# The down product of the ConvFFN as seven block products over pairs of token tiles, with the weight rows in three groups

## The reference

```
def conv_ffn(h, conv_state, w_up, w_conv, b_conv, w_down):
    u = h @ w_up                                   # (T, 1024) @ (1024, 5632)
    ...                                            # causal depthwise convolution of width 3 over tokens
    a, g = jnp.split(uc, 2, axis=-1)
    out = (jax.nn.silu(a) * g) @ w_down            # (T, 2816) @ (2816, 1024)
    return out, padded[:, -(CONV_W - 1):]
...
    x = x + g2 * f_out
```

## Time and profile before

| what | value |
|---|---|
| median of three runs | 3029.07 us |
| the profiled execution's own time, as the page gives it: its span | 3031.5 us |
| TensorE busy | 2948.6 us, 97% |
| VectorE busy | 1759.8 us, 58% |
| ScalarE, GpSimd busy | 1207.0 and 586.9 us |
| matmuls of the down product on TensorE | the first starts at 2504.5, the last at 3020.1 us |

### The profile page before, as it was taken

One profiled execution on the slowest core, in us unless ns is written; L12 is line 12 of the kernel. 1 busy time (PEld: TensorE's weight loads), 2 busy tenths in 40 slices (PEclk: granted clock), 3 DMA queues, 4 the chain that ended last, 5 costly groups with the idle time before them and its releaser, 6 DMA issues.

```text
span 3031.5 us, 48232 instructions
## 1 busy us (share of the span) xinstructions
PE 2948.6 (97%) x17353; PEld 2562.3 (85%) x17353; DVE 1759.8 (58%) x2649; ACT 1207.0 (40%) x2325; POOL 586.9 (19%) x609
## 2 busy tenths in 40 slices
PE   7999999999999999899998999999999999999998
PEld 5878888887777888888888999999999998887886
DVE  2300016733998999795667777777877775234222
ACT  4611112223776888454554333333423233113110
POOL 3310003312666777220110000000000000002000
PEclk8999999999999999999999999999999999999999
DMA  6322224544522251796654444444666676335331
GB/s 217 112 79 73 72 70 157 159 133 112 132 58 58 59 103 36 233 322 204 197 181 171 154 152 153 153 150 157 189 208 217 207 235 233 130 116 186 130 127 55
DMA packets 321026, 446.38 MB, mean 147 GB/s; under 512 B 68994, under 2 KB 220360, under 8 KB 314086
## 3 DMA queue, kind: packets, MB, share of 16 engines
q1 hardware_dynamic: 304616, 394.94, 41.1%
q0 software_dynamic: 14928, 49.38, 4.8%
q10 hardware_dynamic: 1332, 0.06, 0.0%
HBM read 289.20 MB, written 155.10 MB: 147 GB/s over the span
## 4 chain that ended last, share of the span: by engine, by line
PE 51%; DVE 4%; DMA 2%; issue 1%; ACT 1%; SPq 0%; DVEq 0%; ACTq 0%; POOL 0%
PE facc L2600 26%; PE dacc L2709 15%; PE eacc L2579 6%; DMA w_out_plain<-w_out 1%; PE mpT L2726 1%; PE mpm L2735 1%; PE eyT L2562 0%; PE mpS L2745 0%; PE exT L2592 0%; DVE drows L2306 0%; PE mpT L2776 0%; DVE fV L2238 0%; DMA fraw<-w_up 0%; DMA dring<-w_down 0%; PE mpN L2761 0%
## 5 line engine op out<-in xcount | busy, mean ns | idle before, releaser
L2709 PE MATMUL dacc<-drows,dact 128*128 128x512 f32 (+1 forms) x2200 | 511.1, 394 | 4.7 <-DVE dact L2312 1.2
L2709 PEld LDWEIGHTS dacc<-drows,dact 128*128 128x128 f32 (+1 forms) x2200 | 407.8, 186 | 107.6 <-POOL drows L1783 3.2
L767 PE MATMUL pacc<-pring,h1H 128*128 128x512 f32 x1360 | 431.9, 394 | 3.4 <-ACT h1H L326 3.4
L2600 PE MATMUL facc<-fright,fsums 128*128 128x416 f32 x2112 | 417.8, 353 | 9.6 <-ACT facc L1846 6.6
L2600 PEld LDWEIGHTS facc<-fright,fsums 128*128 128x128 f32 x2112 | 398.0, 189 | 15.4 <-issue 7.3
L1123 DVE TENSOR_TENSOR_SCAN aC<-aB,aC,a 128x512 f32<-128x512 f32 (+3 forms) x326 | 362.8, 1113 | 12.1 <-ACT aB L1079 1.1
L1183 POOL TENSOR_TENSOR aS<-aS,aC 128x512 f32<-128x512 f32 (+3 forms) x326 | 335.1, 1036 | 151.9 <-DVE aC L1123 145.5
L767 PEld LDWEIGHTS pacc<-pring,h1H 128*128 128x128 f32 x1360 | 256.8, 189 | 56.2 <-ACT h1H L326 3.5
L2600 PE MATMUL facc<-fright,fwH 128*128 128x416 f32 x1056 | 290.2, 356 | 8.8 <-DVE fU L2222 6.9
L1750 POOL DMA_DIRECT2D y_out<-dy x34 | 18.5, 543 | 1383.3 <-DVE dy L2329 1383.3
L767 PE MATMUL pacc<-pring,h1L 128*128 128x512 f32 x640 | 248.0, 389 | 0.0
(11 more groups left out here) (329 smaller groups left out, 4976.7 us busy)
## 6 DMA issues: line engine op xcount, KB each, us to landing
sums_d<-fsums SPq DMA_DIRECT2D x88, 512.0 KB, 2.9
fsums<-sums_d SPq DMA_DIRECT2D x88, 512.0 KB, 4.7
dact_plain<-act_d SPq DMA_DIRECT2D x32, 1408.0 KB, 6.4
fraw<-w_up SPq DMA_DIRECT2D x66, 512.0 KB, 4.1
proj_out<-pstage SPq DMA_DIRECT2D x119, 256.0 KB, 2.0
qk_T<-pturn POOLq DMA_DIRECT2D x68, 256.0 KB, 3.1
mwa<-w_ada SPq DMA_DIRECT2D x16, 1024.0 KB, 6.8
aq<-qk_T SPq DMA_DIRECT2D x28, 512.0 KB, 11.9
```

The lines of the kernel that those rows point to most:

```text
L767: op = mm_(acc[:, n % NB], h[:, kk, tok(t)], weight(q, w), start=(j == 0), stop=(j == len(order) - 1))
L2600: mm = nc.tensor.matmul(bank, a[:, kk], b[:, kk], start=(begins and kk == 0 and m == 0), stop=(kk == count - 1 and m == 2), skip_group_che ...
L2709: mm = nc.tensor.matmul(down_acc[0:rows, n % 2], at[:, l, kk, 0:rows], r, start=(kk == 0 and m == 0), stop=(kk == NF - 1 and m == len(pass ...
```

## The change

The sixteen prompt tiles are taken in pairs (p, p + 8), the output columns in halves, and the weight rows in three groups of 6, 8 and 8 blocks (GROUPS; half of a group is s = 3, 4, 4 blocks). For one group and one pair the product is a 2 by 2 block product, which Strassen's scheme does in seven products instead of eight. That is a "unit"; there are 3 x 8 = 24 (UNITS), group by group. A product of a unit has 3s matmuls of 128x512, all into one PSUM bank.

Left operands of a unit are A11, A12, A22 and four sums S1 to S4 of activation blocks, each 128 x (128s): VectorE makes the sums (left_sum_of), ScalarE the high and VectorE the low halves, a unit ahead. Right operands ("cells") of a group are B11, B21, B22 and T1 to T4, four sums of weight blocks, each 128 x (512s). GpSimd makes T1 to T4 (first_sums for group 0, next_sum for the others), ScalarE the high halves, VectorE the low halves (for group 0, GpSimd those of T3 and B22, cell_rest). The cells of the next group are made in the last unit of a group (change) and in the first of the next (changed).

ScalarE copies pass the banks on (down_seed_b, down_seed_c, take_five). finish_out gates a result out of PSUM; a partial result is added by GpSimd (add_residual) onto the residual, which is loaded from x1_d and stored there again for each of the three groups, the last time to y_out. SyncE issues all of them. The activations of unit w + 2 are loaded when all low halves of unit w + 1 are made, since all units but unit 1 use one buffer (part). VectorE's convolution and product of the last up tile move into unit 0. The sample is multiplied in plain fp32: 88 matmuls (sample_down, after units 4, 6 and 13), 32 rows each, four of them side by side in the columns of the array with 256 output columns each.

```diff
@@ shapes, orders and places @@
-    NR = 6
-    ND = 2 * NT
-    SWITCH = NT
+    GROUPS = ((0, 3), (6, 4), (14, 4))
+    HALF = NPT // 2
+    UNITS = len(GROUPS) * HALF
+    UP = 2 * NF
+    PRODUCTS = ("P1", "P5", "P6", "P2", "P7", "P3", "P4")
...
@@ SyncE: a unit's loads and stores @@
+            def load_act(w):
+                g, p, k0, s = unit(w)
+                if w == 2:
+                    sp.wait_ge(left_low, 7)
+                elif w > 2:
+                    sp.wait_ge(left_low, 7 * w)
+                to = part_first if w == 1 else part
+                for e in range(2):
+                    sp.dma_start(to[:, e, 0:2 * s], d["act_d"][p + HALF * e, :, k0:k0 + 2 * s, :]).then_inc(part_in, 16)
+            def load_res(w, j):
+                at_least(sp, res_stored[j], 16 * w)
+                rows_, cols_ = out_place(w, j)
+                sp.dma_start(res_of(w, j), d["x1_d"][rows_, cols_]).then_inc(res_in[j], 16)
+            def store_out(w, j):
+                if w == UNITS - 1 and j > 1:
+                    sp.wait_ge(last_out, j - 1)
+                else:
+                    sp.wait_ge(out_ready, 4 * w + j + 1)
+                rows_, cols_ = out_place(w, j)
+                sp.dma_start(d["y_out" if unit(w)[0] == 2 else "x1_d"][rows_, cols_], res_of(w, j)).then_inc(res_stored[j], 16)
...
+                store_out(w, 0)
+                store_out(w, 1)
+                if w + 1 < UNITS:
+                    load_res(w + 1, 0)
+                store_out(w, 2)
+                if w + 1 < UNITS:
+                    load_res(w + 1, 1)
+                if w + 2 < UNITS:
+                    load_act(w + 2)
+                store_out(w, 3)
+                if w + 1 < UNITS:
+                    load_res(w + 1, 2)
+                    load_res(w + 1, 3)
@@ GpSimd @@
+            def add_residual(w, j):
+                if w == UNITS - 1 and j > 1:
+                    return
+                pool.wait_ge(down_gated, 4 * w + j + 1)
+                pool.wait_ge(res_in[j], 16 * w + 16)
+                nc.gpsimd.tensor_tensor(res_of(w, j), res_of(w, j), y2_of(w, j), ALU.add).then_inc(out_ready, 1)
+            def first_sums():
+                sub = lambda to, x, y: nc.gpsimd.tensor_tensor(to, x, y, ALU.subtract)
+                t1, t2, t3, t4 = (cells_plain[f"T{n}"][:, :, 1] for n in range(1, 5))
+                pool.wait_ge(first_blocks_in, 144)
+                for n in range(3):
+                    op = sub(t1[:, n], b12_rows[n], cells_plain["B11"][:, n, 1])
+                op.then_inc(cell_sum, 1)
+                pool.wait_ge(b22_in, 48)
+                pool.wait_ge(cell_sum, 1)
+                pool.wait_ge(done["P6"], UP)
+                sub(cell("T2", 0)[2], cell("B22", 0)[2], cell("T1", 0)[2]).then_inc(cell_sum, 1)
...
+            def cell_rest(name, g):
+                pool.wait_ge(cell_high, 7 * g + HIGHS[g].index(name) + 1)
+                pool.wait_ge(cell_sum, 4 * g + 4)
+                top, low, _ = cell(name, g)
+                nc.gpsimd.tensor_tensor(low, cell_source(name, g), top.bitcast(F32), ALU.subtract).then_inc(cell_low_pool, 1)
+            def next_sum(n, g):
+                sub = lambda to, x, y: nc.gpsimd.tensor_tensor(to, x, y, ALU.subtract).then_inc(cell_sum, 1)
+                if n == 0:
+                    pool.wait_ge(sample_done, g + 1)
+                    pool.wait_ge(done["P5"], UP + HALF * g)
+                    sub(cell("T1", g)[2], raw_block("B12", g), raw_block("B11", g))
+                elif n == 1:
+                    pool.wait_ge(cell_sum, 4 * g + 1)
+                    pool.wait_ge(done["P6"], UP + HALF * g)
+                    sub(cell("T2", g)[2], raw_block("B22", g), cell("T1", g)[2])
+                elif n == 2:
+                    pool.wait_ge(cell_sum, 4 * g + 2)
+                    pool.wait_ge(*low_of("B11", g))
+                    sub(raw_block("B11", g), raw_block("B21", g), cell("T2", g)[2])
+                else:
+                    sub(raw_block("B12", g), raw_block("B22", g), raw_block("B12", g))
+            def down_slot(w):
+                g, p = unit(w)[0:2]
+                change = p == HALF - 1 and g + 1 < len(GROUPS)
+                if change:
+                    next_sum(0, g + 1)
+                    next_sum(1, g + 1)
+                add_residual(w, 0)
+                if change:
+                    next_sum(2, g + 1)
+                add_residual(w, 1)
+                add_residual(w, 2)
+                if change:
+                    next_sum(3, g + 1)
+                add_residual(w, 3)
...
+            first_sums()
+            cell_rest("T3", 0)
+            cell_rest("B22", 0)
+            for w in range(UNITS):
+                down_slot(w)
@@ ScalarE @@
+            def down_seed_b(w):
+                act.wait_ge(done["P1"], UP + w + 1)
+                at_least(act, down_gated, 4 * w)
+                copy(down_b, down_a).then_inc(seeded_b, 1)
+            def take_five(w):
+                act.wait_ge(done["P5"], UP + w + 1)
+                act.wait_ge(c12_taken, UP + w)
+                act.wait_ge(c22_taken, UP + w)
+                copy(five(w), down_e).then_inc(e_taken, 1)
+            def down_seed_c(w):
+                act.wait_ge(done["P6"], UP + w + 1)
+                act.wait_ge(c12_taken, UP + w)
+                copy(down_c, down_b).then_inc(seeded_c, 1)
+            def down_slot(w):
+                g, p = unit(w)[0:2]
+                change = p == HALF - 1 and g + 1 < len(GROUPS)
+                changed = p == 0 and g > 0
+                down_seed_b(w)
+                if changed:
+                    cell_high_of("T3", g)
+                take_five(w)
+                if change:
+                    cell_high_of("B11", g + 1)
+                down_seed_c(w)
+                if changed:
+                    cell_high_of("B22", g)
+                if w + 1 == UNITS:
+                    return
+                for name in LEFTS:
+                    if name == "S3":
+                        if w == 0:
+                            silu(UP - 1, NARROW)
+                        if change:
+                            cell_high_of("T1", g + 1)
+                    elif name == "S4" and change:
+                        cell_high_of("B21", g + 1)
+                    elif name == "A22" and change:
+                        cell_high_of("T2", g + 1)
+                    elif name == "A12" and changed:
+                        cell_high_of("T4", g)
+                    left_high_of(name, w + 1)
@@ VectorE @@
...
+            def left_sum_of(n, w):
+                at = act_blocks(w)
+                s1, s2, s3, s4 = (left(f"S{m}", w)[2] for m in range(1, 5))
+                if n == 1:
+                    dve.wait_ge(part_in, 32 * w + 32)
+                    dve.wait_ge(done["P5"], UP + w)
+                    op = v.tensor_tensor(s1, at["A21"], at["A22"], ALU.add)
+                elif n == 2:
+                    dve.wait_ge(done["P2" if w == 0 else "P6"], UP + w)
+                    dve.wait_ge(left_sum, 4 * w + 1)
+                    op = v.tensor_tensor(s2, s1, at["A11"], ALU.subtract)
...
+                op.then_inc(left_sum, 1)
+            def left_low_of(name, w):
+                dve.wait_ge(left_high, 7 * w + LEFTS.index(name) + 1)
+                if name in ("S1", "S2"):
+                    dve.wait_ge(left_sum, 4 * w + (2 if name == "S1" else 4))
+                top, low, own = left(name, w)
+                v.tensor_tensor(low, own if name[0] == "S" else act_blocks(w)[name], top.bitcast(F32), ALU.subtract).then_inc(left_low, 1)
...
+            def finish_out(w, j):
+                y_ = y2_of(w, j)
+                gate_ = down_gate[:, out_place(w, j)[1]]
+                dve.wait_ge(done[("P2", "P7", "P3", "P4")[j]], UP + w + 1)
+                at_least(dve, out_ready, 4 * w + j - 1)
+                if j in (0, 3):
+                    v.tensor_tensor(y_, down_a if j == 0 else down_b, gate_, ALU.mult).then_inc(down_gated, 1)
+                else:
+                    sem = c22_taken if j == 1 else c12_taken
+                    dve.wait_ge(e_taken, UP + w + 1)
+                    v.tensor_tensor(y_, down_b if j == 1 else down_c, five(w), ALU.add).then_inc(sem, 1)
+                    dve.wait_ge(sem, UP + w + 1)
+                    v.tensor_tensor(y_, y_, gate_, ALU.mult).then_inc(down_gated, 1)
...
+            def down_slot(w):
+                g, p = unit(w)[0:2]
+                n = w + 1
+                more = n < UNITS
+                change = p == HALF - 1 and g + 1 < len(GROUPS)
+                changed = p == 0 and g > 0
+                if changed:
+                    cell_low_of("T3", g)
+                if more:
+                    left_sum_of(1, n)
+                    left_sum_of(2, n)
+                if change:
+                    cell_low_of("B11", g + 1)
+                if more:
+                    left_low_of("A11", n)
```

(64 more changed lines are left out.)

488 lines of the change are left out of this document (270 added, 218 removed).

## The result

The changed kernel takes 3069.95 us (median of 4 runs, 3067.53 to 3073.33) against 3030.07 (4 runs, 3028.74 to 3033.63): a ratio of 1.013, 95% interval 1.0115 to 1.0144. It is slower, as forecast, but by 40 us where 9 were forecast (3038 against 3029), and the time lies above the range (2966 to 3062).

A forecast was written before the change was run, and what follows sets the result against it. TensorE, busy 97%, was taken to set the time. Matmuls and waits, 426.2 + 3 + 20 + 15.5 + 27 + 24 + 6 + 5 = 526.7 us, gave 3038 in all, own range 3023 to 3056, with rivals 2966 to 3062.

The forecast's parts named there:

- matmuls at their own pace: Down product on TensorE: 1848 matmuls replace 2112, at 0.2306 us each, 426.2 us against 487.0.
- (a): Joint of up and down products: TensorE waits for GpSimd's and VectorE's first cells, which exclude each other; 20 us, bounds 3.4 to 22.
- (b): Group 0: one-buffer ring of activation load and VectorE work takes 17.2 us a unit against 14.5; 15.5 us, bounds 0 to 25.
- the sample elsewhere: Sample's 88 plain fp32 matmuls, two of three groups standing where TensorE waits anyway: 3 us, bounds 0 to 30.
- (c): First change of group, units 7 and 8: VectorE's and GpSimd's port work adds up to 50.4 us; costs 27, bounds 8 to 30.
- (d): Second change of group: the same 50.4 us of port work, costing 24 us, bounds 6 to 27.
- (e): Ring in groups 1 and 2: 19.5 us a unit plus semaphores against 19.4, over 14 rounds; 6 us, bounds 0 to 25.
- (f): Slow clock after TensorE's long waits at the joint and changes: three times 3.4, half counted; 5 us, bounds 0 to 10.
- The rest: Small items outside the main terms: up product's last tiles 1 us, tail 8.0 instead of 11.0, raw weight rows 0, at most 4.
- The first: Rival for the whole down product: VectorE and GpSimd hardly disturb each other, time 2963 us; chance 0.25.
- The second: Rival for the down product's waits: 60 us instead of 97.5, gaps having been double counted, time 3001; chance 0.17.
- The third: Rival for the activation ring: longer, with load 6.4 and more adds, units 19 and 21 us, time 3063; chance 0.16.

The follow-up runs named there:

- E1: Changed kernel with the transfers of w_down's rows issued earlier, by GpSimd's queue instead of SyncE's: 3057.9 us (ratio 1.0092).
- E6: E1 plus a second, earlier requested buffer for group 0's activations and conv_out's transfers on GpSimd's queue: 3043.3 us (1.0048).
- E2: Changed kernel with GpSimd's four sums at each change of group nearly left out (16 of 512 columns written): 3040.9 us (1.0036).
- E3: Changed kernel with GpSimd's residual adds nearly left out (16 of 512 columns written), all waits kept: 3047.1 us (1.0056).
- E9: E6 and E7 together, VectorE's and ScalarE's work at changes reordered, T1's and T2's sums first, adds VectorE's only in units 7, 8, 15, 16: 3020.0 us (0.9958).
- E10: E9 with the sums of T1 to T4 and all residual adds back on GpSimd, the new order kept: 3033.8 us (1.0012).
- E4: Changed kernel with the sample's product keeping only each group's first and last block, row transfers and waits kept: 3066.7 us (1.0125).
- E7: Changed kernel with the four sums at each change and all units' residual adds moved from GpSimd to VectorE: 3067.3 us (1.0124).
- E5: Changed kernel with each of GpSimd's 2048-column sums at the changes issued as four of 512 columns, nothing left out: 3064.8 us (1.0112).

## Why the prediction was right and wrong

The sign was right, and so was the mechanism: the waits ate more than TensorE saved, and the largest lie where they were forecast, before P6 of units 8 and 16, named VectorE (15.25 and 15.24 us). The size was off by 32 us. Step by step, in us:

```
term                                    forecast  measured  difference
matmuls at their own pace                 426.2     430.5      +4.3
(a) joint, unit 0 above steady             20        15.6      -4.4
(b) group 0, units 1 to 6, with sample     15.5+     35.4
    the sample elsewhere                   3          3.7     +20.6
(c) first change                           27        33.7      +6.7
(d) second change                          24        30.5      +6.5
(e) units 9 to 14 and 17 to 23             6          3.9      -2.1
(f) clock (measured: inside a to d)        5          -        -5
start of the product                     2505.5    2507.2      +1.7
its end to the span's end                  8.0        5.5      -2.5
span against median                       -2.4       +4.0      +6.4
```

(Measured terms are sums of the unit times above, less 14.75 or 19.53 a unit; (e) is without the 3.7 of the sample's matmuls in unit 13.)

**The step that failed** is one sentence under "The rest", which left the rows out of the sum and out of the ring of term (b): "The loads of raw weight rows (3 to 4 MB) lie well ahead of their use: 0, at most 4." They do lie ahead of their use. What they hold up is other transfers that are under way with them: a residual's store (9.0 us instead of 2.5), for which SyncE stands, and the activations of the next unit, which group 0's ring of one buffer has no slack for. E1, which moved and advanced these loads, took 12.0 us less, 9.9 of it in units 4, 6 and 11, and the disturbance was not gone. The ring's own length was right: forecast 17.2, and where no rows are under way the transfer of some 5.2 and the 11.9 from the first sum to the last low half (2587.50 to 2599.37) make 17.1; E6 took it away and units 3 to 6 stood at 14.6 to 15.9 without the sample. But the sign that units 2 to 6 would be spaced 17 us did not come: they took 24.1, 14.8, 26.3, 14.8 and 26.8, 21.3 on average. And one wait the prediction didn't have at all: ScalarE's 8.05 us for conv_out's transfer, behind which TensorE waited 4.70 us before P7 of unit 2, with 2.6 of slow clock after it. Unit 2 fell by 3.9 in E6, where that transfer was moved together with the second buffer. The rows and this wait are 12 and some 4 us of the 32; most of the rest is in (c), (d) and the span.

**(c), (d), the size of GpSimd's work.** Right in kind, too small in size. The page by shape for the down product:

```profile
L1867 POOL TENSOR_TENSOR dres<-dres,dy 128x512 f32<-128x512 f32 x86 | 149.9, 1743 | 303.3 <-DVE dy L2581 234.2 <-DVE dy L2587 69.0
L1898 POOL TENSOR_TENSOR draw_rows<-draw_rows,dT_plain 128x2048 f32<-128x2048 f32 x2 | 10.0, 5022 | 0.0
```

A sum took 4.9 on average where I had drawn the line through 432 and 1188 ns on to 4.2, and an add mostly 1.53 or 1.65 where those rows said 1.19 (median 1.67; two of 86 took 1.28). Four of one and four of the other, at 1.53, are 2.8 + 1.4 = 4.2 us more a change. That gives 31 and 28. The slow clock, which had a term of its own, adds more than the 2.5 and 2.3 that are left (5.3 and 5.7 by the lengths of the products), so the parts don't fit to the last us. Of the changes' 64 us, E2 gives the sums 30 and E3 the adds 14 (no run leaves out both), and E9 and E10 say that moving both to VectorE is worth 14 of them once VectorE's order lets it start in time.

**(f) the clock.** I had 5 us. Twelve products of the changed kernel have a granted clock of 0.50 to 0.74 and take 0.7 to 2.5 us longer than the same product elsewhere (2.96 for one of 12, 2.26 for one of 9), as the 3.76 and 5.09 above and unit 4's 3.66. Each stands behind a wait of TensorE, of 2.2 to 15.3 us, but for one right behind such a product. Added up, 19.1 us. They are inside a to d: not three pauses had this price, as I had counted, but eleven, five of them in the joint and group 0 (8.2 us) and six at the changes (10.9). With it the product's time is nearly all named: 430.5 of matmuls, 10.1 of the sample, 87.7 of waits and 19.1 of slow clock are 547.4 of 553.3 us. No run here shows what the time would be with the waits and without this price.

**The sample.** 3 us was right by the units: E4 left out 64 of the 88 matmuls and only unit 13 fell, by 2.9, although 10.1 us of them stand in TensorE's rows (32 matmuls in 3.66 us). Two of the three groups stand where VectorE is late in any case. That holds while those waits last: in E6, without them, units 4 and 6 are longer than their neighbours by 3.3 and 4.8.

**(a) and (e)** were forecast a little too long. **Pace:** the 0.2306 came from steps of 66 matmuls into one bank; products of 9 and 12 in a row take 0.2341 and 0.2325 a matmul. The 86.8% that the prediction calls the work left is a slip (1848 of 2112 is 87.5%); its sum doesn't use it. **Span and median:** the profiled execution of before lay 2.4 above its median, that of after 4.0 below its own; 6.4 us of the miss is this, the scatter of single executions and not a step of the argument.

**Rivals.** The first (no exclusion, 2963) is refuted by the 4.90, 6.67 and 3.80 us rows. The second (waits of 60, 3001) is out by the 87.7. The third (a longer ring, 3063) came nearest by its number, but that is luck: it has a slower load and more adds in every unit, and the ring in groups 1 and 2 stood at 19.53, with 3.9 us above it in thirteen units; the cost was in units 2, 4 and 6 of group 0.

What stays open: how the 19.1 us of slow clock would fall if only the waits before them were shortened; what the exclusion costs apart from the length of GpSimd's work; and the first unit's 15.6 us, which no run took apart (E3 took 0.9 of them). TensorE's rows say where they lie: waits of 0.7, 4.1, 4.9 and 2.7 us before P5, P6, P2 and P4, and 2.5 of slow clock.

## What to carry to other kernels

A large load that nobody needs soon still delays the small transfers beside it, in its own queue and, less, from another one (a store landed in 9.0 and 7.1 us instead of 2.5); before placing such loads, look for a ring with one buffer. Another queue and an earlier request for the loads gave 12.0 us here, a second buffer with an earlier request for the ring 14.6 more (with conv_out's transfers moved). Where two engines shut each other out, add up both engines' time at the tightest place, put the work on the engine that does it faster (2.28 against 4.9 us here), and then check the order: E7 had the right sum and gained nothing, because the first step of the chain stood behind a wait that had nothing to do with it. And a scheme that saves matmuls has to be priced by the units in which the others are late: 87.5% of the matmuls, and still 37 us longer in the down product; E9, with the same 1848 matmuls, has it in 505.2 us.

## What the runs showed of the hardware beyond what was expected

- Four sums of 512 columns take GpSimd 6.6 to 9.9 us beside VectorE's work at the first change (8.0 for T1's, E5), one of 2048 columns 4.6 to 5.0 in the changed kernel: the exclusion changes hands between operations, and pieces make each engine's wait shorter and the whole sum longer.
- Plain fp32 matmuls in four column tiles of 32 do overlap: four records of 379 to 404 ns start within 21 ns, and 64 records of 256 columns take 3.66 us, 57 ns a record (each matmul counts as two, so 114 ns a matmul, forecast 120).
- After a wait of 15.25 us the first product of 12 matmuls took 5.09 us (granted clock 0.56, mostly 1.2 GHz); a product at a granted clock of 1.00 (2.4 GHz) takes 2.96.
- A store of 256 KB, issued 3 us after 3 MB of rows in the same queue, landed after 9.0 us and kept its successor waiting 6.4; the median of such stores in the down product is 2.5 to landing. With the rows on another queue and asked for earlier it was 7.1 and 4.6.
